# The samples' paged attention moved out of a stage of its own, into the mixer and the output projection of the prompt

## The chip, the core and the metric

The kernel runs on one core of one Trainium2 chip. The metric is the device time of one execution in microseconds (us). Before the change it is 3100.78 us, the median of three runs (3095.70 to 3108.07). Lower is better.

Engines: PE (TensorE, matrix products), ACT (ScalarE), DVE (VectorE), POOL (GpSimd), SP (SyncE, which here only issues transfers). Each works through its own list of instructions in the written order; they wait for one another by semaphores.

## The reference, cut to what matters

One inference step of a decoder with two layers, for a prompt group (1024 tokens) and a sample group (8 sequences of one new token). All is float32. In each layer:

```
h   = rmsnorm(x) * (1 + sc1) + sh1
aq, ak, av, af, bq, bk, bv, bg, ca, cb = split(h @ w_in)
o_a = attention of 4 heads x 128      (prompt: causal; samples: over 256 past rows + the new one)
o_b = retention, 4 heads x 64;  o_c = gated causal convolution, width 31
x   = x + g1 * rmsnorm(concat(o_a, o_b, o_c) @ w_o)
x   = x + g2 * rmsnorm(ffn(rmsnorm(x) ...))           (1024 -> 2 x 2816 -> 1024)
```

The change concerns the attention of the samples, which reads its past from pages (16 pages of 128 rows x 4 heads x 128, that is two for each of 8 samples), named by a page table:

```
k_all  = concat(cache_k[page_table], k_new);  v_all, lf_all likewise
cum    = cumsum(lf_all)
logits = (q . k_all) * scale + cum[new] - cum[key]
out    = softmax(logits) @ v_all              for 8 samples x 4 heads = 32 rows
```

## The kernel before

The program is a sequence of blocks; between two blocks all engines meet at a barrier. For each layer: `block_modulation`, `block_project`, `block_mixer`, `block_samples`, `block_tail`. Token columns are 1032: 1024 of the prompt and, at the end, 8 of the samples (`TP:NT`).

**Products in two parts.** Operands of the large products are split in a high and a low part (ACT writes `hi`, DVE or POOL subtracts for `lo`), and each product is three matmuls: hi x hi, lo x hi, hi x lo.

**`block_mixer`.** A loop over 42 *passes* (`p`), each a third of the columns for one of 14 weight tiles of `w_in`: 24 matmuls on `dense`. Between two passes PE does a step of the attention, which runs 9 passes behind: `phase(p)` gives the head `h` and the step `at`. So `p = 14` is head 0, step 5, `p = 23` head 1, step 5, `p = 37` head 3, step 1. Scores lie in the bank `sc`, DVE takes the top (`top_of`), ACT the exponential, DVE divides (`normalize`), PE transposes (`turn_probs`), ACT moves, PE multiplies with the values (`values`, into `o_bank`), DVE copies (`out_of`). SP loads the weight tiles in order (`load`, each waits until the tile two before it has been split) and stores K and V (`store`). `k.x` does not hold the residual here: it is parked in DRAM (`x_hold`), and its place holds q, k, v and the probabilities. `q_new`, `k_new`, `v_new` are the samples' columns, copied by `new_token`. In passes 1 to 12 DVE also does the last taps of the convolution (semaphore `tapped`).

**`block_samples`.** The samples' attention alone. SP loads 16 K pages and half of the V pages, ACT the 16 `lf` pages (log forget) and the other V pages. POOL spreads the query (`qd`), PE repeats it over all partitions (`q_bank`), DVE multiplies with K (`prod`) and sums (`lg`): 8 times. PE adds the bias (`b_bank`), turns the logits to 32 rows (`r_bank`), DVE and ACT do the softmax, PE turns it back (`t_bank`, `n_bank`) and multiplies: 16 matmuls with the weights in `pt` and 512 columns of V moving (`so_bank`), then four to turn the result (`q_bank`). Beside it SP loads and ACT and POOL split the first two tiles of `w_o` (`Ahead`), and SP loads the residual back into `k.x`.

**`block_tail`.** The output projection, then the feed-forward part, in two *halves* of the tokens: half 0 is 512 columns, half 1 is 520 with the samples. In half 0 and then half 1 PE goes through 8 *tiles* of `w_o` (`out_tile(hf, m)`, 24 matmuls in half 0, hooks `out_hook` before each `kk`). ACT runs `split(0)`, splits weight tile 2 (`high_to(2)`), then `split(1)`, then for each tile `finish(hf, m)`: square, copy, split the weight tile three ahead. DVE runs `lower(0)`, `lower(1)`, then `add_square`. Weight tiles pass through three buffers (`Stream`); SP loads them in order. `turn_context` (L1884) is a row of small matmuls between tiles 2 and 3. `joins[hf]` add the result to `k.x` later, in the time of the next half.

The places that the change and the steps below touch: `block_mixer` (L730; spread queries, K pages, two more weight tiles), `block_samples` (L1395, whole), `block_tail` (L1794; SP's list, `out_hook`, the ACT and DVE lists of half 0).

## Time and profile before

| what | us |
|---|---|
| median of three runs | 3100.78 |
| the profiled execution, whole | 3097.88 |
| its span, first to last instruction | 3096.1 |
| PE busy / DVE busy / ACT busy | 2880.4 / 1739.7 / 1171.4 |
| `block_samples` with its barriers, layer 0 (603.90 to 657.05) | 53.15 |
| the same, layer 1 (2130.00 to 2183.40) | 53.40 |
| half 0 of the output projection, layer 0 (657.05 to 712.00) | 54.95 |

The span is 1.78 us shorter than the execution. The mean granted TensorE clock is 0.948 of full speed. A matmul of float32 by float32 leaves two MATMUL records, one on split operands leaves one. A record's duration is a latency: matmuls overlap, so what a row of them costs is read from where the next row starts.

### The profile page before, as it was taken

Reading aid. Unit: us, or ns where it says so; the run is one execution under the profiler, and the core shown is the slowest. Engines: PE = TensorE matmul, PEld = TensorE weight load, DVE = VectorE, ACT = ScalarE, POOL = GpSimd, SP = SyncE. Lnnn points to the kernel's source line nnn. Section 1 sums busy time; section 2 is a strip of 40 time slices with the busy share of each in tenths; the row PEclk is TensorE's granted clock in tenths of the full one; section 3 lists DMA queues with packets and bytes.
Section 4 is the critical chain, followed back from the end, with each engine's and each line's share of the span. In section 5 each row is a group of like instructions: output and inputs, shape, how many; then the busy total and the mean of one; then the engine's idle time right before and its main releaser. Section 6 shows DMA issues by size and latency. Waiting matters only on the chain. (4 is left out here: it accounts for less than half of the span.)

```text
span 3096.1 us, 44175 instructions
## 1 busy us (share of the span) xinstructions
PE 2880.4 (93%) x17804; PEld 2467.3 (80%) x17804; DVE 1739.7 (56%) x2809; ACT 1171.4 (38%) x1863; POOL 335.9 (11%) x166
## 2 busy tenths in 40 slices
PE   6799999889999999999767999997999999999996
PEld 3587888658778889999726878885788788999995
DVE  1286433336676676676614944334266767676765
ACT  1222233424444445444312413333344444444442
POOL 4112010123000000000042210101320000000000
PEclk7799999989999999999868999997999999999998
DMA  8313111162323233323191221114422333332231
GB/s 313 132 41 107 36 35 35 50 200 79 95 89 95 89 96 96 89 89 96 38 341 51 92 49 36 35 28 144 137 75 89 96 96 92 92 96 89 89 96 65
DMA packets 366881, 293.29 MB, mean 95 GB/s; under 512 B 24189, under 2 KB 308389, under 8 KB 365886
## 3 DMA queue, kind: packets, MB, share of 16 engines
q1 hardware_dynamic: 355472, 284.18, 29.2%
q10 hardware_dynamic: 11214, 6.41, 0.7%
q8 instruction: 135, 2.21, 0.3%
q14 instruction: 60, 0.49, 0.1%
HBM read 267.68 MB, written 23.71 MB: 94 GB/s over the span
## 5 line engine op out<-in xcount | busy, mean ns | idle before, releaser
L1643 PE MATMUL tslot<-g_hi,w_hi 128*128 128x260 f32 (+1 forms) x2496 | 673.3, 324 | 7.6 <-DVE g_lo L2172 6.0
L1643 PE MATMUL tslot<-g_hi,w_lo 128*128 128x260 f32 (+1 forms) x2496 | 667.4, 322 | 0.0
L1643 PE MATMUL tslot<-g_lo,w_hi 128*128 128x260 f32 (+1 forms) x2496 | 665.4, 321 | 0.0
L1643 PEld LDWEIGHTS tslot<-g_hi,w_hi 128*128 128x128 f32 x2496 | 416.5, 190 | 48.7 <-DVE g_lo L2172 6.2
L1643 PEld LDWEIGHTS tslot<-g_hi,w_lo 128*128 128x128 f32 x2496 | 415.6, 190 | 38.0
L1643 PEld LDWEIGHTS tslot<-g_lo,w_hi 128*128 128x128 f32 x2496 | 415.8, 190 | 37.6
L1614 ACT ACTIVATE w_hi<-w_raw 128x1024 fp32r<-128x1024 f32 x292 | 307.1, 1052 | 317.5 <-PE tslot L1961 312.6
L2233 DVE TENSOR_TENSOR cat<-cat,tslot 128x512 f32<-128x512 f32 (+1 forms) x320 | 220.6, 690 | 192.1 <-PE tslot L1961 190.8
L1618 DVE TENSOR_TENSOR w_lo<-w_raw,w_hi 128x1024 fp32r<-128x1024 f32 x256 | 312.0, 1219 | 0.0
L1961 PE MATMUL tslot<-f_hi,w_hi 128*128 128x260 f32 (+1 forms) x1056 | 283.3, 323 | 6.0 <-DVE w_lo L1618 3.7
L1961 PE MATMUL tslot<-f_hi,w_lo 128*128 128x260 f32 (+1 forms) x1056 | 281.9, 322 | 0.0
L1961 PE MATMUL tslot<-f_lo,w_hi 128*128 128x260 f32 (+1 forms) x1056 | 280.9, 320 | 0.0
L2196 DVE SCALAR_TENSOR_TENSOR bufs<-bufs,vecs 128x512 f32<-128x512 f32 x176 | 132.1, 750 | 235.2 <-ACT bufs L2097 235.2
L854 PE MATMUL dense<-h_hi,w_hi 128*128 128x344 f32 x672 | 231.0, 344 | 5.3 <-PEq L2384 5.3
L854 PE MATMUL dense<-h_hi,w_lo 128*128 128x344 f32 x672 | 216.5, 322 | 0.0
L854 PE MATMUL dense<-h_lo,w_hi 128*128 128x344 f32 x672 | 216.4, 322 | 0.0
L1961 PEld LDWEIGHTS tslot<-f_hi,w_hi 128*128 128x128 f32 x1056 | 175.4, 190 | 26.9 <-DVE cat L2233 5.5
L1961 PEld LDWEIGHTS tslot<-f_lo,w_hi 128*128 128x128 f32 x1056 | 175.7, 189 | 16.0
L1961 PEld LDWEIGHTS tslot<-f_hi,w_lo 128*128 128x128 f32 x1056 | 176.2, 190 | 14.7
L505 DVE SCALAR_TENSOR_TENSOR cat<-cat,vecs 128x1023 f32<-128x1023 f32 (+14 forms) x120 | 176.3, 1469 | 3.3
L154 PE MATMUL slot<-h_hi,w_hi 128*128 128x260 f32 x528 | 119.6, 337 | 34.0 <-POOL h_lo L454 15.6
L2097 ACT ACTIVATE bufs<-bufs,vecs 128x520 f32<-128x520 f32 (+1 forms) x176 | 144.2, 820 | 18.2
(317 smaller groups left out, 4029.7 us busy)
## 6 DMA issues: line engine op xcount, KB each, us to landing
w_raw<-in_ffn_up_dram SPq DMA_DIRECT2D x176, 512.0 KB, 3.7
a_raw<-in_ada_w_dram SPq DMA_DIRECT2D x24, 2048.0 KB, 18.6
w_raw<-in_ffn_down_dram SPq DMA_DIRECT2D x88, 512.0 KB, 3.6
w_raw<-in_w_in_dram SPq DMA_DIRECT2D x46, 512.0 KB, 3.9
w_raw<-in_w_o_dram SPq DMA_DIRECT2D x32, 512.0 KB, 4.0
x_hold<-x_res SPq DMA_DIRECT2D x2, 4128.0 KB
x_res<-x_hold SPq DMA_DIRECT2D x2, 4128.0 KB, 16.0
kp<-in_cache_k_dram SPq DMA_DIRECT2D x32, 256.0 KB, 3.0
```

The costliest lines, as they stand in the source:

```text
L154: last = e.matmul(out[:, OFF + a:OFF + b], w[:, k, cols], x[:, k, a:b], start=(k == 0 and first), stop=(k == kt - 1 and w is w_lo))
L505: return dve.scalar_tensor_tensor(acc, u[:, 0:TP - CTX + w], k.vecs[:, 1, 2 * w + j:2 * w + j + 1], acc, ALU.mult, ALU.add)
L854: last = pe.matmul(dense[p % 2][:, 0:b - a], w[:, kk, :], x[:, kk, a:b], start=(kk == 0 and first), stop=(kk == KD - 1 and w is w_lo))
L1614: act.activation(self.hi[n % 3][:, :, :], self.raw[n % 3][:, :, :], ACT.Copy).then_inc(self.hi_done, 1)
L1618: e.tensor_tensor(self.lo[n % 3][:, :, :], self.raw[n % 3][:, :, :], self.hi[n % 3][:, :, :].bitcast(F32), ALU.subtract).then_inc(self.dve ...
L1643: last = pe.matmul(out[:, at + a:at + b], w[:, kk, :], x[:, kk, t0 + a:t0 + b], start=(kk == 0 and first), stop=(kk == KD - 1 and w is w_lo))
L1961: last = pe.matmul(out[:, at + a:at + b], w, x[e][:, a:b], start=first and name == pairs[0], stop=final and name == pairs[-1])
L2097: act.activation(t_ab[half][:, 0:w], raw[half][:, 2:2 + w], ACT.Identity, scale=vec[:, 3, c:c + 1], bias=vec[:, 3, c + 2 * FT:c + 2 * FT + ...
L2196: dve.scalar_tensor_tensor(tt[:, 0:512], r[:, 1:513], tap1, tt[:, 0:512], ALU.mult, ALU.add).then_inc(conv, 1)
L2233: dve.tensor_tensor(y_m, y_m, out[:, at:at + w], ALU.add).then_inc(gathered, 1)
```

## The change

`block_samples` is gone. Its work is spread over its two neighbours:

- **In the mixer.** The queries are repeated by PE from `q_new` itself (`spread_query`, four matmuls 128x128, one sample each), at eight passes, for one head and four samples at a time; DVE multiplies and sums there. K pages are loaded for one head at a time (16 transfers of 128 rows x 512 bytes), into a part of `k.cat` and, for head 3, of `k.x`, by SP between the weight tiles. The first two tiles of `w_o` pass through the mixer's own weight loop as tiles 14 and 15.
- **In half 0 of the output projection.** SP loads the 16 `lf` pages ahead of the weight tiles and the 16 V pages behind tile 4; PE's bias, rows, probabilities and values hang in `out_hook` at tiles 1, 2, 4 and in the middle of 5. The values are now 64 matmuls with V as the weights and one column moving. ACT and DVE take the small steps between tiles. The samples' columns of the first four groups of `k.cat` are split last (`split_samples`, `sample_low`), and half 1 waits for them (`samp_lo`).
- **The residual** returns in two transfers, by token half, in half 1, after the values are done, each with a semaphore (`x_back`).

```diff
@@ block_mixer
+        both_att = sb("att", [P, 2, 2, 2 * P])
+        att = [both_att[:, i, :, :] for i in range(2)]
+        prod = both_att[:, :, :, :].rearrange("p a b c -> p a (b c)")
+        pages = [k.cat[:, 4:6, 0:S * DA]] * 3 + [arena[:, 0:4 * NT].rearrange("p (a b) -> p a b", b=NT)[:, 0:4:2, 0:S * DA]]
+        SPREADS = {14: (0, 0), 20: (0, 1), 23: (1, 0), 29: (1, 1), 32: (2, 0), 33: (2, 1), 37: (3, 0), 38: (3, 1)}
...
+            def load_keys(h):
+                if h == 0:
+                    sp.wait_ge(tapped, 2 * CONV_W - TAPS_EARLY)
+                elif h < 3:
+                    sp.wait_ge(prod_done, 2 * h)
+                else:
+                    sp.wait_ge(scored, NC8 * 3)
+                    sp.wait_ge(turned, 9)
+                    sp.wait_ge(new_done, 9)
+                for n in range(S * NPG):
+                    sp.dma_start(pages[h][:, n % NPG, DA * (n // NPG):DA * (n // NPG) + DA],
+                                 d["cache_k"][L, bass.ds(page(n), 1), :, h, :].rearrange("o p n -> p (o n)")).then_inc(k_loaded[h % 2], 16)
...
-            for n in range(5, N_TILES):
+            for n in range(5, N_TILES + 2):
                 load(n)
+                if n in (6, 9, 12, 13):
+                    load_keys({6: 0, 9: 1, 12: 2, 13: 3}[n])
...
+            sp.wait_ge(lo_done, N_TILES + 1)
...
+                    if i == 0 and h in (1, 2):
+                        pe.wait_ge(prod_done, 2 * h)
...
+                    if i == 4 and h < 2:
+                        pe.wait_ge(prod_done, 2 * h + 1)
...
+            def spread_query(p):
+                h, half = SPREADS[p]
+                ph, at = phase(p)
+                pe.wait_ge(new_done, 3 * h + 2)
+                if h >= 2:
+                    pe.wait_ge(g_scaled, 12)
+                    pe.wait_ge(prod_done, 2 * h + half)
...
+                for j in range(4):
+                    s = 4 * half + j
+                    last = pe.matmul((x_bank if h >= 2 else o_bank)[:, P * j:P * j + P], k.q_new[:, h, s:s + 1].to_broadcast([P, P]), ident,
+                                     start=True, stop=True)
+                last.then_inc(q_spread, 1)
...
-                    if p % 3 == 2 and p // 3 + 2 < N_TILES:
+                    if p % 3 == 2:
                         high(p // 3 + 2)
...
+            def multiply(p):
...
+                dve.wait_ge(q_spread, 2 * h + half + 1)
+                dve.tensor_tensor(prod, pages[h][:, :, 512 * half:512 * half + 512], bc((x_bank if h >= 2 else o_bank)[:, :], 1, NPG),
+                                  ALU.mult).then_inc(prod_done, 1)
...
+            def reduce(p):
...
+                dve.tensor_reduce(k.lg[:, :, 4 * half:4 * half + 4, h], prod.rearrange("p g (s n) -> p g s n", n=DA), AX_X,
+                                  ALU.add).then_inc(lg_done, 1)
@@ block_samples: all removed
@@ block_tail, SP
             sp.dma_start(stage, d["state_ffn_conv"][L].rearrange("s r (c n) -> c (s r) n", n=P)).then_inc(s_ready, 16)
+            for n in range(S * NPG):
+                page = sp.value_load(k.pages[0:1, n:n + 1], min_val=0, max_val=N_POOL - 1)
+                sp.dma_start(lf[:, n // NPG, n % NPG, :], d["cache_logf"][L, bass.ds(page, 1)].rearrange(
+                    "o p h -> p (o h)")).then_inc(lf_loaded, 16)
...
+                    if (hf, m) == (0, 4):
+                        for n in range(S * NPG):
...
+                    if (hf, m) in ((1, 1), (1, 5)):
+                        back = int(m == 5)
+                        sp.wait_ge(v_summed, 1)
+                        sp.dma_start(k.x[:, :, joins[back].all], k.x_hold.rearrange("p (a b) -> p a b", b=NT)[:, :, joins[back].all]).then_inc(
+                            x_back[back], 16)
@@ block_tail, PE
+            def sample_bias():
+                ones, after = const(k, "ones"), const(k, "after")
+                pe.wait_ge(e_ready, 1)
+                pe.wait_ge(lf_loaded, 16 * S * NPG)
...
+            def sample_values():
+                pe.wait_ge(pt_moved, 1)
+                pe.wait_ge(v_loaded, 16 * S * NPG)
+                for h in range(HA):
+                    for s in range(S):
+                        for pg in range(NPG):
+                            last = pe.matmul(slot[2][:, BANK + S * h + s:BANK + S * h + s + 1], vp[:, s, pg, DA * h:DA * h + DA],
+                                             pt[:, pg, HA * s + h:HA * s + h + 1], start=(pg == 0), stop=(pg == NPG - 1))
+                last.then_inc(v_summed, 1)
...
+                    if (hf, m, kk) == (1, 0, 0):
+                        pe.wait_ge(samp_lo, 1)
+                    if hf == 0:
+                        step = {(1, 0): sample_bias, (2, 0): sample_rows, (4, 0): sample_probs, (5, 4): sample_values}.get((m, kk))
@@ block_tail, ACT
             for m in range(KD):
                 finish(0, m)
+                if m == 2:
+                    exp_samples()
...
+                if m == 6:
+                    split_samples()
@@ block_tail, DVE
             lower(0)
+            sample_bias()
             lower(1)
+            sample_logits()
             for m in range(1, KD):
                 add_square(0, m)
+                if m == 2:
+                    sample_top()
+                elif m == 3:
+                    sample_normalize()
+                elif m == 4:
+                    sample_turned()
+                elif m == 5:
+                    sample_out()
+                elif m == 7:
+                    sample_low()
+            dve.wait_ge(x_back[0], 16)
```

**SP at the start of the tail.** The list of SP before, layer 0: the context of the convolution, then the weight tiles of `w_o`.

```order
L131 DMA w_raw<-in_w_o_dram 128x8x128 x2
L1442 DMA x_res<-x_hold 128x8256
L1399 UNCONDITIONAL_BRANCH
L1847 UNCONDITIONAL_BRANCH
L1849 DMA rc<-in_state_ffn_conv_dram 44x16x128
L1604 DMA w_raw<-in_w_o_dram 128x8x128 x6
```

And after the change; the five rows from TENSOR_LOAD to DMA stand 16 times for `lf`, and 16 times in the same form for V:

```order
L1771 DMA rc<-in_state_ffn_conv_dram 44x16x128
L1773 TENSOR_LOAD pages
L1773 ISA x2
L1774 ISA
L1774 DMA bufs<-in_cache_logf_dram 128x4
...
L1512 DMA w_raw<-in_w_o_dram 128x8x128 x3
L1782 TENSOR_LOAD pages
...
L1783 DMA x_res<-in_cache_v_dram 128x512
L1512 DMA w_raw<-in_w_o_dram 128x8x128 x3
```

The first weight tile that the tail loads (tile 2) now stands behind 16 page loads.

**PE in half 0, the samples' last product.** Before it stood in a block of its own:

```order
L1473 MATMUL t_bank<-consts,rows 128x32 x2
L1474 MATMUL n_bank<-dnew,consts 128x32
L1481 MATMUL so_bank<-vpg,pt 32x512 x16
L1486 MATMUL q_bank<-consts,orow 128x8 x4
```

After the change it stands in the middle of tile 5:

```order
L1551 MATMUL tslot<-g_hi,w_hi 128x512
L1551 MATMUL tslot<-g_lo,w_hi 128x512
L1551 MATMUL tslot<-g_hi,w_lo 128x512
L1864 MATMUL tslot<-bufs,x_res 128x1 x64
L1551 MATMUL tslot<-g_hi,w_hi 128x512
```

Sixteen matmuls with 512 moving columns have become 64 with one, each with 128 columns of new weights.

**DVE in the mixer at pass 14 (head 0, step 5).** Before:

```order
L1290 TENSOR_SCALAR nb<-mx 128x1
L1308 SCALAR_TENSOR_TENSOR cat<-x_bank,cat 128x384
L1295 RECIPROCAL rr<-rs 128x1
L1297 TENSOR_SCALAR prob<-prob,rr 128x896
L1267 COPY q_new<-x_res 128x8
```

After:

```order
L1340 TENSOR_SCALAR nb<-mx 128x1
L1358 SCALAR_TENSOR_TENSOR cat<-x_bank,cat 128x384
L1407 TENSOR_TENSOR att<-cat,o_bank 128x1024
L1345 RECIPROCAL rr<-rs 128x1
L1347 TENSOR_SCALAR prob<-prob,rr 128x896
L1413 TENSOR_REDUCE lg<-att 128x2x4
L1317 COPY q_new<-x_res 128x8
```

The product stands ahead of the division by the row sum, the reduction behind it.

## Rows read from the trace of the kernel before

**Rows 1.** Windows by stage: length, PE busy (instructions), granted clock, DMA share, GB/s.
```profile
274.00:603.90 329.90, 325.48 (x2152) 0.99 0.14 38
603.90:657.05 53.15, 34.35 (x78) 0.74 0.75 258
657.05:712.00 54.95, 53.51 (x226) 0.91 0.38 106
...
2130.00:2183.40 53.40, 35.26 (x78) 0.71 0.74 257
```

**Rows 2.** Timeline, DVE, samples' stage: start, length, line, operation, idle before it.
```profile
603.57 0.29 DVE L1302 COPY cat<-o_bank 128x128 f32<-128x128 f32 x1 [4.58 <-PE o_bank L993]
605.18 0.19 DVE L1519 TENSOR_TENSOR e_new<-consts,logf 128x32 f32<-128x32 f32 x1 [1.32 <-PEq L2384]
...
612.92 1.21 DVE L1527 TENSOR_TENSOR prod<-kp,q_bank 128x1024 f32<-128x1024 f32 x1
614.17 1.22 DVE L1529 TENSOR_REDUCE lg<-prod 128x8 f32<-128x1024 f32 x1
```

**Rows 3.** Timeline of SP, the samples' stage and the start of the tail.
```profile
606.14 16.95 SPq L1436 DMA_DIRECT2D kp<-in_cache_k_dram  x16
...
657.05 0.37 SPq L1849 DMA_DIRECT2D rc<-in_state_ffn_conv_dram  x1
657.47 20.03 SPq L1604 DMA_DIRECT2D w_raw<-in_w_o_dram  x6
```

**Rows 4.** Window of 20 us in the mixer, PE alone.
```profile
560.00:580.00 20.00, 20.00 (x133) 1.00 0.18 54
```

**Rows 5.** Timeline of PE in the mixer, the attention steps around pass 35.
```profile
541.10 0.93 PE L979 MATMUL turn<-consts,prob 128*128 128x128 f32 x7
...
545.65 1.72 PE L993 MATMUL o_bank<-x_res,v_tok 128*128 128x128 f32 x14
547.21 1.04 PE L979 MATMUL turn<-consts,prob 128*128 128x128 f32 x8
```

**Rows 6.** Timeline of DVE in the mixer at passes 12 to 14.
```profile
372.86 1.25 DVE L505 SCALAR_TENSOR_TENSOR cat<-cat,vecs 128x994 f32<-128x994 f32 x1
...
393.73 0.56 DVE L1308 SCALAR_TENSOR_TENSOR cat<-x_bank,cat 128x384 f32<-128x384 f32 x1
394.91 0.16 DVE L1295 RECIPROCAL rr<-rs 128x1 f32<-128x1 f32 x1 [0.62 <-ACT prob L1138]
```

**Rows 7.** DMA issues: size of one, median us to landing.
```profile
kp<-in_cache_k_dram SPq DMA_DIRECT2D x32, 256.0 KB, 3.0
```

**Rows 8.** Timeline of ACT, start of the tail and finish of tile 3.
```profile
657.08 4.27 ACT L2037 ACTIVATE g_hi<-cat 128x512 fp32r<-128x512 f32 x8 [2.72 <-PEq L2384]
663.63 1.06 ACT L1614 ACTIVATE w_hi<-w_raw 128x1024 fp32r<-128x1024 f32 x1 [2.28 <-DMA w_raw<-in_w_o_dram]
...
689.69 0.60 ACT L2051 ACTIVATE bufs<-tslot 128x512 f32<-128x512 f32 x1 [10.56 <-PE tslot L1643]
```

**Rows 9.** Timeline of PE around `turn_context`, layer 0.
```profile
676.99 4.71 PE L1884 MATMUL tmisc<-consts,rc 44*128 44x44 f32 x32
681.63 0.79 PE L1643 MATMUL tslot<-g_hi,w_hi 128*128 128x512 f32 x1
```

**Rows 10.** Windows there; columns PE, PEld, DVE, ACT, POOL busy, then granted clock.
```profile
677.00:679.60 2.60, 2.60 (x25) 2.60 (x24) 0.69 (x1) 2.03 (x3) 0.50 (x2) 1.00 0.65 169
679.60:681.60 2.00, 2.00 (x11) 1.95 (x10) 0.00 (x0) 0.00 (x0) 1.95 (x1) 0.50 0.55 191
681.60:686.40 4.80, 4.80 (x12) 3.80 (x12) 0.00 (x0) 0.00 (x0) 0.00 (x0) 0.50 0.37 109
```

**Rows 11.** Windows of line L391, modulation; columns PE, PEld busy, granted clock.
```profile
101.90:102.75 0.85, 0.85 (x8) 0.85 (x8) 1.00 0.00 0
102.75:104.35 1.60, 1.60 (x10) 1.60 (x9) 0.50 0.00 0
```

**Rows 12.** Timeline of PE in the mixer, line L873.
```profile
281.62 2.03 PE L873 MATMUL o_bank<-cat,prob 64*64 64x1 f32 x64
```

More of the change, by code:

```diff
@@ L835, in _ @@
                 plink(pool.tensor_tensor(pre[:, HA * c:HA * c + HA], pre[:, HA * c - HA:HA * c], k.logf[:, HA * c - HA:HA * c], ALU.add))
-            for n in range(1, N_TILES):
+            for n in range(1, N_TILES + 2):
                 pool.wait_ge(hi_done, n)
@@ L1803, in block_tail @@
         diag = sb("diag", [P, 520])
-        v, y, t = (sb(n, [P, 5]) for n in ("jv", "jy", "jt"))
+        v, y, t = (k.ncum[:, 8 * n:8 * n + 5] for n in range(3))
         hs = diag[:, 0:KD * S].rearrange("p (k s) -> p k s", s=S)
@@ L1814, in block_tail @@
         ring, acc = [rc[:, i, :] for i in range(3)], rc[:, 3, :]
+        R = S * HA
+        vp = k.x[:, :, :].rearrange("p a b -> p (a b)")[:, 0:S * NPG * HA * DA].rearrange("p (s g n) -> p s g n", s=S, g=NPG)
+        lots = [raw[0][:, 2 + a:2 + b] for a, b in ((0, 257), (257, 289), (289, 321), (321, 385), (385, 417), (417, 449), (449, 453), (453, 517))]
+        rows, dnew, one = lots[0][0:R], lots[4][0:R], lots[6][0:R]
+        e_new, qk, vn = (lots[i].rearrange("p (s h) -> p s h", h=HA) for i in (1, 2, 5))
+        lf = lots[7].rearrange("p (s g h) -> p s g h", s=S, g=NPG)
+        pt = lots[3].rearrange("p (g r) -> p g r", g=NPG)
+        (v_loaded, lf_loaded, e_ready, b_ready, lg_ready, qk_ready, rows_ready, rows_link, neg_ready, exp_done, prob_ready, pt_ready, pt_moved,
+         v_summed, cat_done, samp_hi, samp_lo) = (k.sem(n) for n in (
+             "v_loaded", "lf_loaded", "e_ready", "b_ready", "lg_ready", "qk_ready", "rows_ready", "rows_link", "neg_ready", "exp_done",
+             "prob_ready", "pt_ready", "pt_moved", "v_summed", "cat_done", "samp_hi", "samp_lo"))
+        x_back = [k.sem(f"x_back{i}") for i in range(2)]
+        N_POOL = d["cache_v"].shape[1]
         st = Stream(k, k.w_raw, k.w_hi, k.w_lo)
@@ L2034, in split, with split_samples, exp_samples @@
             def split(hf):
-                cols = joins[hf].all
                 for kk in range(KD):
+                    cols = joins[hf].cols if kk < HA else joins[hf].all
                     act.activation(k.h_hi[:, kk, cols], k.cat[:, kk, cols], ACT.Copy).then_inc(x_hi, 1)
+            def split_samples():
+                act.wait_ge(cat_done, 1)
+                act.activation(k.h_hi[:, 0:HA, TP:NT], k.cat[:, 0:HA, TP:NT], ACT.Copy).then_inc(samp_hi, 1)
+            def exp_samples():
+                act.wait_ge(neg_ready, 1)
+                act.activation(rows, rows, ACT.Exp, bias=one[:, 1:2], accum_out=one[:, 2:3]).then_inc(exp_done, 1)
             def finish(hf, m):
@@ L2168, in lower @@
             def lower(hf):
-                cols = joins[hf].all
                 for kk in range(KD):
+                    cols = joins[hf].cols if kk < HA else joins[hf].all
                     dve.wait_ge(x_hi, KD * hf + kk + 1)
@@ new lines, in sample_logits, with sample_top @@
+            def sample_logits():
+                dve.wait_ge(b_ready, 1)
+                flat = k.lg[:, :, :, :].rearrange("p g s h -> p (g s h)")
+                dve.scalar_tensor_tensor(flat, flat, A_SCALE, slot[2][:, 0:NPG * R], ALU.mult, ALU.add).then_inc(lg_ready, 1)
+            def sample_top():
+                dve.wait_ge(rows_ready, 1)
+                link(dve.tensor_copy(rows[:, 0:PAST], slot[2][0:R, BANK:BANK + PAST]))
+                link(dve.tensor_scalar(rows[:, PAST:PAST + 1], slot[2][0:R, BANK + PAST:BANK + PAST + 1], A_SCALE, None, ALU.mult))
+                link(dve.tensor_reduce(one[:, 0:1], rows, AX_X, ALU.max))
+                dve.tensor_scalar(one[:, 1:2], one[:, 0:1], -1.0, None, ALU.mult).then_inc(neg_ready, 1)
@@ new lines, in sample_normalize, with sample_turned @@
+            def sample_normalize():
+                dve.wait_ge(exp_done, 1)
+                link(dve.reciprocal(one[:, 3:4], one[:, 2:3]))
+                dve.tensor_scalar(rows, rows, one[:, 3:4], None, ALU.mult).then_inc(prob_ready, 1)
+                dve.wait_ge(prob_ready, 1)
+                dve.tensor_scalar(dnew, const(k, "ident")[0:R, 0:R], rows[:, PAST:PAST + 1], None, ALU.mult).then_inc(prob_ready, 1)
+            def sample_turned():
+                dve.wait_ge(pt_ready, 1)
+                dve.tensor_copy(pt, slot[2][:, 0:NPG * R].rearrange("p (g r) -> p g r", g=NPG)).then_inc(pt_moved, 1)
+                link(dve.tensor_tensor(vn, k.v_new[:, :, :].rearrange("p h s -> p s h"),
+                                       slot[2][:, 2 * R:3 * R].rearrange("p (s h) -> p s h", h=HA), ALU.mult))
@@ new lines, in sample_out, with sample_low @@
+            def sample_out():
+                dve.wait_ge(v_summed, 1)
+                dve.tensor_tensor(k.cat[:, 0:HA, TP:NT], vn.rearrange("p s h -> p h s"),
+                                  slot[2][:, BANK:BANK + R].rearrange("p (h s) -> p h s", h=HA), ALU.add).then_inc(cat_done, 1)
+            def sample_low():
+                dve.wait_ge(samp_hi, 1)
+                dve.tensor_tensor(k.h_lo[:, 0:HA, TP:NT], k.cat[:, 0:HA, TP:NT], k.h_hi[:, 0:HA, TP:NT].bitcast(F32),
+                                  ALU.subtract).then_inc(samp_lo, 1)
```

212 lines of the change are left out of this document (58 added, 154 removed).

## The prediction

> **What bounds the kernel now.** I read the page first (busy shares, the slices), then windows by stage, then the timelines of the engines where the change cuts. PE is busy 93% of the span, so the question at each place is whether PE waits or works. The windows say where it does not work: in the mixer it is busy 325.5 of 329.9 us at a granted clock of 0.99, in the samples' stage 34.35 of 53.15 us (35.26 of 53.40 in layer 1) at 0.74 and 0.71, in half 0 of the output projection 53.51 of 54.95 [rows 1]. The two samples' stages, 106.55 us, are what there is to win. Both neighbours are bound by PE: 20 us in the mixer hold 20.00 us of PE [rows 4]. Whatever PE gets there lies on the path; whatever DVE, ACT or SP get may be hidden. The chain that ended last covers only the output of the result and says nothing here.
>
> The sum is made against the profiled execution, 3097.88 us (span 3096.1 and 1.78 around it); it lies 2.9 under the median of 3100.78.
>
> **Removed.** Stage and barriers, 53.15 and 53.40. One barrier stays: from the mixer's last copy, 603.57 + 0.29, to the first instruction of the next block, 605.18, that is 1.32 us [rows 2]. So 51.8 + 52.1 = 103.9 us go. With them goes the waiting for K, since K is now loaded passes ahead, and the transfer of the residual, which returns in the time of half 1 and isn't needed before the joins there: nothing is charged for it unless v_summed is late, and even then the first half (2 MB) has 15 us and more.
>
> **Mixer, added on PE.** Eight spreads per layer, each 4 matmuls of 128 columns with new weights, 8 records. Fourteen such records take 547.21 - 545.65 = 1.56 us, 0.111 each [rows 5]; a spread is 0.9 and with the change of operands 0.95 us. Eight are 7.6. PE has no idle time there, so all of it counts. The high parts of tiles 14 and 15 are two ACT instructions of 1.06 us [rows 8]; the second falls where the last head runs without passes to hide it, and I add 0.7. Mixer: 8.3 per layer, 16.6 in all. Bounds: nothing for the second term, 2 for late steps: 15 to 19, if DVE stays hidden.
>
> **Mixer, added on DVE and SP, taken as nothing.** A product is 1.21 and a reduction 1.22 us [rows 2], 16 pairs in all, 38.9 us. What hides them: at pass 14 DVE sits idle for 0.62 us ahead of the reciprocal while ACT does the exponential [rows 6], and what it makes there PE wants only after the next pass, some 3.8 us of matmuls (541.10 plus 7 x 0.11, to 545.65) [rows 5]. K of head 0 is issued when the last tap is done, 372.86 + 1.25 = 374.1 [rows 6]; sixteen page loads take 16.95 us [rows 3] and land 3.0 later [rows 7]: 394.1, against a product that starts near 394.8. Heads 1 and 2 have three passes as well, 20 us for 20. So there is no slack worth the name in the loads, but what is late by a microsecond delays DVE, not yet PE. If the cover is gone, each pair costs up to 2.43 us.
>
> **Half 0, step by step (layer 0, from SP's first transfer at 657.05).** What one tile takes: tile 3 runs from 681.63 [rows 9] to about 689.6, where ACT reads it [rows 8]; 4.8 us of it at half clock [rows 10], which cost 2.4. At full clock a tile is 5.6 us. Tiles 1 and 2 before 676.99 give the end of tile 0: 665.8, or 8.7 on this count.
>
> 1. *The wait for lf.* Sixteen page loads with their register loads took 16.95 us, (16.95 - 0.37)/15 = 1.10 each [rows 3]. Behind the first transfer they end near 17.7, and land near 20.5. PE stands at the head of tile 1 from 8.7 on: 11.8 us. Then it is cold: the bias' 10 records at 0.21 are 2.1, tile 1 loses 2.4. Together 16.3. The first weight tile for SP, tile 2, comes behind the same loads: issued 17.7, split by ACT from 23.9 (6.2 from issue to ACT, as 657.47 to 663.63 [rows 3, 8]), then 1.06, the split of half 1 like the 4.27 of half 0, and 1.1 for finish: 30.3. PE ends tile 1 at 30.6. So this second wait lies beside the first, and to take away one alone would gain little.
> 2. *Rows.* 6 records, 1.0.
> 3. *Probabilities.* DVE normalizes only after the square of tile 3: ACT 0.6, DVE some 0.7 for the addition (0.56 for 384 columns [rows 6]), then three small instructions. PE waits 2.5, then 6 records, 1.0: 3.5.
> 4. *Values.* 64 matmuls are 128 records, each with 128x128 of new weights and one column. The row nearest in form is L391: 8 records in 0.85 us at 2.4 GHz, 0.106 each; at 1.2 GHz 9 weight loads in 1.60, 0.18 each [rows 11]. In turn_context, 24 or 25 records take 2.6 us at full clock, and the last 8 the 2.0 us to 681.63, 0.25 each [rows 9, 10]. I take 0.11 and 0.21. Which clock? In turn_context PE and its weight loads were busy all the time (2.60 of 2.60), and the clock fell to 1.2 GHz after 2.6 us, and stayed there for 4.8 us of the next tile [rows 10]. So: about 3 us at full clock (27 records), 101 x 0.21 = 21.2, together 24.2; then 2.4 lost in the rest of tile 5. 26.6. Bounds: 128 x 0.11 = 14.1 with no loss after, and 128 x 0.25 + 2.4 = 34.
> 5. *The samples' low part.* Half 1 waits until tile 7 is squared, added, and the samples' columns subtracted: 1.9.
>
> Sum 16.3 + 1.0 + 3.5 + 26.6 + 1.9 = 49.3 per layer, 98.6 for two. The V loads (16 x 1.10 us on SP behind tile 4) end near 36, long before values at about 61, and weight tile 5 behind them is there near 40, wanted at 58.
>
> By the page "TensorE: Matmul & The Clock Gate" of the Trainium skill, section "What's actually happening", the clock follows how busy PE has been recently. Taken as busy share, that would keep it high in the values, and give the second case below; the row with PE and weight loads at 100% and a falling clock speaks against it. The same page, section "LDWEIGHTS (loading the stationary operand)", has a weight load cost its columns over 1.2, in ns, whatever the rows: 107 ns for 128. At full clock the trace agrees (0.106); at half it shows about twice that, so the rule's 13.7 us for the values is again the case of the clock that stays.
>
> **Total.** -103.9 + 16.6 + 98.6 = +11.3: 3109.2, rounded up for small waits to 3110. The whole stage removed is paid back, three quarters of the repayment (85.8 of 115.2 us) by two things: SP's page loads ahead of the weights, and matmuls that load 128 columns of weights to move one.
>
> **Rivals.**
> - *The clock stays high in the values.* Condition: weight loads count as work. For it: nothing in the trace shows so long a row of such records; against it, the fall in a short one [rows 10]. Values 14.1 in place of 24.2, no 2.4 after: -12.5 per layer, 3085.
> - *Small weight loads are cheaper.* 64 records with 64x64 weights took 2.03 us, 0.032 each [rows 12]; by that rate values are 4 us. These use a quarter of the array, and L391 has the right form, so it is unlikely. -22.6 per layer: 3065.
> - *The lf loads don't hold PE.* Condition: a page load alone on SP is much quicker than beside ACT's (both queues issued at once in the stage before). At half the pace the wait is some 8 us shorter; the whole of it with its cold start is 14.2. Between -16 and -28: 3088.
> - *DVE becomes the mixer's bound (the slow side).* Place: the division of the row sums behind the product, above all at passes 20, 29 and 38 where two are divided, and where K arrives late. It decides from the point where the division ends later than the pass that covers it: over about 3.8 us. Only the product stands ahead of the division: 16 x 1.21 = 19: 3129; with the reductions 3149. Against it: the idle time ahead of the reciprocal [rows 6] takes half a product.
>
> **How the numbers follow.** Forecast 0.62 (3110, own range 3098 to 3122); clock stays 0.12; cheap loads 0.03; lf quick 0.06; DVE bound 0.17. 0.5% of the median is 15.5 us, about what can be told from no change: faster is under 3085.3, slower over 3116.3. Faster: half of the second case and the lf case, the cheap loads, some mixtures: 0.18. Slower: a fifth of the forecast, and the DVE case: 0.29. Same: 0.53. Range 3080 to 3130: down to the clock case with part of the lf case, up to the product in the mixer's path.
>
> **What would show it.** After: no window between mixer and tail but a barrier of 1.3 us. In the tail, PE idle for about 12 us behind its first 24 matmuls, released by lf transfers; a row of 128 records with one column of about 24 us with a clock that falls after 3; half 0 near 104 us in place of 55. In the mixer, stages of about 338 us, PE still without idle time, spreads of 0.9. It is wrong if PE has idle time in the mixer released by DVE, if the values take 14 us, or if PE waits at tile 1 for much less than 12.

## The result and the profile after

| | us |
|---|---|
| before, 20 runs | 3096.22 (3092.26 to 3108.07) |
| after, 20 runs | 3111.20 (3102.34 to 3119.93) |
| ratio | 1.0044, interval 1.0034 to 1.0053 |
| forecast | 3110, range 3080 to 3130 |

The change costs 15.0 us by the medians. It is small, but the interval excludes equality. Against the 3100.78 of the first three runs, it is 10.4 us; the two profiled executions (3097.88 and 3108.57) differ by 10.7.

The stages after, as in [rows 1] (length, PE busy and its instructions, granted clock, DMA share, GB/s); the kernel after has no window between mixer and tail:

```profile
271.70:609.90 338.20, 333.26 (x2216) 0.99 0.19 53
611.15:718.36 107.21, 86.67 (x375) 0.75 0.39 117
1803.70:2141.40 337.70, 333.26 (x2216) 0.99 0.19 53
2142.69:2247.35 104.66, 83.94 (x375) 0.77 0.41 120
```

Between the last mixer instruction and the tail's first lie 1.28 us in either layer. So the balance, measured in the two profiles:

| term | forecast | measured |
|---|---|---|
| samples' stages gone | -103.9 | -104.0 (53.15 + 53.40 - 2 x 1.28) |
| mixer | +8.3 and +8.3 | +8.3 and +5.8 |
| half 0 | +49.3 and +49.3 | +52.5 and +53.0 |
| sum | +11.3 | +15.6 |

Half 0 is measured from SP's first transfer to PE's first matmul of half 1: 611.15 to 718.36 against 657.05 to 711.8, and 2142.69 to 2247.35 against 2183.34 to 2235.0 before. The rest of the program is 4.9 us shorter in the profile of after; no run explains that. It is less than such stretches scatter: from DVE's row `diag` (128x8) in half 1 of layer 0 to SP's first transfer in the tail of layer 1, where after, e2, e3, e7, e10 and e11 have the same code, their profiles have 1310.6 to 1321.4 us.

SP at the start of the tail (the list that answers to [rows 3]), start and length:

```profile
611.15 0.32 SPq L1771 DMA_DIRECT2D rc<-in_state_ffn_conv_dram  x1
612.51 16.91 SPq L1774 DMA_DIRECT2D bufs<-in_cache_logf_dram  x16
629.78 1.86 SPq L1512 DMA_DIRECT2D w_raw<-in_w_o_dram  x3
632.40 17.91 SPq L1783 DMA_DIRECT2D x_res<-in_cache_v_dram  x16
```

PE in half 0 and at the head of half 1, the rows where it waited, and the values:

```profile
630.86 0.60 PE L1837 MATMUL tslot<-bufs,consts 128*128 128x32 f32 x2 [11.13 <-DMA bufs<-in_cache_logf_dram]
644.32 1.03 PE L1847 MATMUL tslot<-consts,lg 128*32 128x128 f32 x4 [4.16 <-DVE lg L2183]
666.33 0.74 PE L1855 MATMUL tslot<-consts,bufs 32*128 32x32 f32 x4 [2.21 <-DVE bufs L2197]
678.64 22.68 PE L1864 MATMUL tslot<-bufs,x_res 128*128 128x1 f32 x128
718.36 0.48 PE L1551 MATMUL tslot<-g_hi,w_hi 128*128 128x260 f32 x2 [1.61 <-DVE g_lo L2212]
```

Four waits, 19.1 us in all (19.3 in layer 1), and a row of 128 records that takes 22.68 us (24.14 in layer 1). The rest of what half 0 got longer is small products, and matmuls at half clock behind each pause.

Windows of the values; columns PE, PEld, DVE, ACT, POOL busy, then granted clock:

```profile
678.60:681.60 3.00, 3.00 (x29) 2.96 (x28) 0.00 (x0) 0.00 (x0) 1.93 (x1) 1.00 0.00 0
681.60:701.20 19.60, 19.60 (x104) 19.60 (x103) 0.00 (x0) 0.00 (x0) 0.00 (x0) 0.55 0.00 1
```

PE never stops, and its clock falls nevertheless: a mean of 0.55 over 19.6 us is 1.0 for the first 2.0 of them and 0.5 (1.2 GHz) for the rest, so it fell some 5 us into the row.

In the mixer at pass 14, DVE (answers to [rows 6]):

```profile
393.25 1.22 DVE L1407 TENSOR_TENSOR att<-cat,o_bank 128x1024 f32<-128x1024 f32 x1 [0.40 <-PE o_bank L1080]
394.39 0.15 DVE L1345 RECIPROCAL rr<-rs 128x1 f32<-128x1 f32 x1
394.58 0.69 DVE L1347 TENSOR_SCALAR prob<-prob,rr 128x896 f32<-128x896 f32 x1
395.18 1.22 DVE L1413 TENSOR_REDUCE lg<-att 128x8 f32<-128x1024 f32 x1
```

The idle time of 0.62 us ahead of the reciprocal is gone: the product takes its place, and the reduction stands behind the division. The reciprocal starts 2.10 us behind the start of the operation of L1358 (392.29), where it was 1.18 before; PE shows no wait between 300 and 560 us all the same.

### The profile page after: what moved, and what is told of

It is laid out like the page before. It is cut to its first block and busy times, and to the rows that moved or that the text cites. A ratio compares the mean times of both kernels' runs of the same rounds, so it can differ in the third digit from the quotient of the medians.

```text
span 3106.8 us, 45241 instructions
## 1 busy us (share of the span) xinstructions
PE 2888.8 (93%) x18076; PEld 2518.0 (81%) x18076; DVE 1742.5 (56%) x2811; ACT 1169.9 (38%) x1863; POOL 317.0 (10%) x148
## 3 DMA queue, kind: packets, MB, share of 16 engines
q8 instruction: 137, 2.24, 0.3%
q10 hardware_dynamic: 4302, 2.15, 0.2%
```

## The experiments

Each edit is against the changed kernel ("after") unless said otherwise. Medians of the comparison's runs:

| kernel | median us | ratio to before | interval |
|---|---|---|---|
| after | 3111.20 | 1.0044 | 1.0034 to 1.0053 |
| lf pages early | 3073.11 | 0.9915 | 0.9902 to 0.9928 |
| weights first | 3116.72 | 1.0065 | 1.0050 to 1.0080 |
| values spread | 3099.38 | 1.0005 | 0.9992 to 1.0018 |
| lf early + values spread | 3067.83 | 0.9898 | 0.9884 to 0.9912 |
| DVE product twice | 3112.32 | 1.0050 | 1.0033 to 1.0068 |
| PE spreads twice | 3125.22 | 1.0092 | 1.0074 to 1.0110 |
| residual whole | 3108.16 | 1.0038 | 1.0025 to 1.0050 |
| residual later | 3104.85 | 1.0029 | 1.0014 to 1.0044 |
| values spread + residual later | 3084.20 | 0.9961 | 0.9946 to 0.9976 |
| lf early + values spread + residual later | 3050.93 | 0.9866 | 0.9842 to 0.9889 |
| the same, two steps later in their tiles | 3043.06 | 0.9830 | 0.9808 to 0.9852 |

**The lf pages early (e1).**

```diff
@@ block_mixer, SP, behind the last store
+            for n in range(S * NPG):
+                sp.dma_start(k.lf[:, n // NPG, n % NPG, :], ...cache_logf...).then_inc(lf_loaded, 16)
+            sp.wait_ge(lf_loaded, 16 * S * NPG)
@@ block_tail, SP
-            for n in range(S * NPG):
-                page = sp.value_load(k.pages[0:1, n:n + 1], min_val=0, max_val=N_POOL - 1)
-                sp.dma_start(lf[:, n // NPG, n % NPG, :], ...).then_inc(lf_loaded, 16)
@@ block_tail, PE, sample_bias
-                pe.wait_ge(lf_loaded, 16 * S * NPG)
```

> The 16 lf pages are loaded by SP at the end of the mixer, into a place of their own, and not at the head of the tail; PE's bias waits for none. My theory: PE's idle time behind its first 24 matmuls in half 0 (11.1 us in layer 0), the cold start after it, and the second wait inside the bias go, in both layers: about 16 us each, 3111 - 32 = 3079. Half 0 falls from 107 to about 91 us. Rival A, the pages only move the wait (the mixer's barrier now waits for them, or PE waits for the weight tile instead): under 5 us in all, 3106 to 3111. Rival B, the idle time costs nothing but itself: 2 x 11.1 = 22, 3089.

Measured: 3073.11, 38 under after and 6 under my theory. PE goes straight from tile 0 to the bias:

```profile
623.56 0.40 PE L1556 MATMUL tslot<-g_hi,w_lo 128*128 128x512 f32 x1
623.79 0.31 PE L1837 MATMUL tslot<-mod,consts 128*128 128x32 f32 x2
```

and half 0 takes 90.30 and 90.93 us, 16.9 and 13.7 shorter than after; the forecast's step 1 had 16.3. That is 30.6 of the 38; the other 7 were not found in a stage (the profiled execution of this kernel, 3080.7 in span, is as slow as the slowest of its five runs). Both rivals fall: the gain is larger than the bare idle time, and the wait does not move to the barrier or the weight tile.

**The weights first (e2).**

```diff
@@ block_tail, SP
-            for n in range(S * NPG):
-                page = sp.value_load(k.pages[0:1, n:n + 1], min_val=0, max_val=N_POOL - 1)
-                sp.dma_start(lf[:, n // NPG, n % NPG, :], d["cache_logf"][L, bass.ds(page, 1)]...).then_inc(lf_loaded, 16)
             for hf in range(2):
...
                     if (hf, m) == (0, 4):
+                        for n in range(S * NPG):
+                            page = sp.value_load(k.pages[0:1, n:n + 1], min_val=0, max_val=N_POOL - 1)
+                            sp.dma_start(lf[:, n // NPG, n % NPG, :], d["cache_logf"][L, bass.ds(page, 1)]...).then_inc(lf_loaded, 16)
```

> The weight tiles 2 to 4 are issued ahead of the lf pages, which now stand behind tile 4, right ahead of the V pages. The prediction said that the wait for weight tile 2 lies beside the wait for lf. My theory: PE still waits for lf at tile 1, and longer (tile 4's transfer waits for a buffer, so lf is issued only when tile 1 is split): as PE's bias stands ahead of tile 1, and the buffer of tile 4 is free once ACT and POOL have split tile 1, which they do at the start, the loads move some 3 to 6 us later: slower by 2 x 3 to 2 x 6, 3117 to 3123. Rival, the late weights are the cost of half 0 and not lf: faster by 10 or more, under 3101.

Measured: 3116.72, 5.5 slower than after, where the two intervals overlap by a hair, and far from the rival's 3101. The wait at the bias is 4.6 us longer, and the wait for the logits behind tile 1 (4.16 in layer 0 of after, 1.36 in layer 1) is gone:

```profile
636.59 0.60 PE L1837 MATMUL tslot<-bufs,consts 128*128 128x32 f32 x2 [15.74 <-DMA bufs<-in_cache_logf_dram]
```

So with lf late, early weights gain nothing in the balance. The edit moves both, and so prices neither alone: the wait for the logits, which my expectation left out, went, and kept the loss at its lower end (half 0 is 106.70 and 106.53 us).

**The values spread (e3).**

```diff
@@ block_tail, PE: 16 groups of 4 matmuls, ahead of kk = 4..7 of tile 5, 0..7 of 6, 0..3 of 7
-                step = {..., (5, 4): sample_values}.get((m, kk))
+                if 0 <= KD * (m - 5) + kk - 4 < 16:
+                    step = sample_values(KD * (m - 5) + kk - 4)
@@ block_tail, DVE
-                elif m == 5:
+                elif m == 6:
                     sample_out()
```

> The 64 matmuls of the values are cut into 16 groups of 4, each ahead of one kk step of tiles 5 to 7, so that 3 matmuls with 512 moving columns stand between two groups. My theory: the granted clock no longer falls, the 128 records take 0.11 us each, 14.1 us in place of 22.7 to 24.2, and tile 5 loses no 2.4 us at half clock: faster by 11 to 12.7 per layer, 3111 - 24 = 3087. The chain to the samples' low part is later by about one tile, which may cost up to 2 per layer. Rival, the price is the number of weight loads with one column whatever the clock: no gain, 3108 to 3114.

Measured: 3099.38, 11.8 under after: half of the forecast, and the interval lies apart from after's. The clock did what the theory said:

```profile
680.00:685.00 5.00, 5.00 (x36) 4.57 (x35) 0.00 (x0) 0.00 (x0) 0.76 (x1) 1.00 0.00 0
685.00:690.00 5.00, 5.00 (x35) 4.55 (x34) 0.69 (x1) 2.03 (x3) 2.38 (x1) 1.00 0.00 0
```

against 0.55 over the same stretch above. Tiles 5 to 7 with the values take 31.2 us (PE's idle time ahead of half 1 not counted); three times the 5.58 of tile 6 in after are 16.7, so the 128 records cost 14.5 us, 0.113 each, instead of 22.5 and a rest of tile 5 at half clock. Half 0 is 96.06 and 96.39 us, 11.1 and 8.3 shorter. But from half 1 of layer 0 to the tail of layer 1 the program is 8.3 us longer, and 4.4 behind half 0 of layer 1. The rows there, POOL and DVE, then PE:

```profile
715.05 2.39 POOL L1526 TENSOR_TENSOR w_lo<-w_raw,w_hi 128x1024 fp32r<-128x1024 f32 x1 [12.42 <-ACT w_hi L1522]
717.97 2.35 POOL L1526 TENSOR_TENSOR w_lo<-w_raw,w_hi 128x1024 fp32r<-128x1024 f32 x1 [0.52 <-ACT w_hi L1522]
```

```profile
714.92 0.17 DVE L164 SCALAR_TENSOR_TENSOR ncum<-ncum 128x4 f32<-128x4 f32 x1
715.12 2.34 DVE L165 SCALAR_TENSOR_TENSOR ncum<-ncum 128x4 f32<-128x4 f32 x1
...
718.09 2.77 DVE L1599 TENSOR_TENSOR diag<-consts,ncum 128x512 f32<-128x512 f32 x1
```

```profile
720.92 1.12 PE L1584 MATMUL tslot<-diag,consts 128*128 128x512 f32 x2 [2.26 <-DVE diag L1599]
```

An instruction on 128x4 elements takes 2.34 us, and ends when POOL's subtraction ends (715.05 + 2.39 = 717.44); the diagonal, 0.69 in after, ends half a microsecond behind the next. Why does POOL work just there? Because ACT split the weight tile late, and it waited for its transfer:

```profile
713.91 1.06 ACT L1522 ACTIVATE w_hi<-w_raw 128x1024 fp32r<-128x1024 f32 x1 [5.51 <-DMA w_raw<-in_w_o_dram]
```

SP had issued the residual's 2 MB at 703.71, ahead of that weight tile's load at 704.38; half 1 began at 708.9. In after the residual is issued at 701.35 and half 1 begins at 718.36, so there was room. The Trainium skill, page "SBUF — State Buffer", section "SBUF: two separate sides", says that DVE and GpSimd share one port pair as an exclusive lock: a DVE instruction with two SBUF inputs, behind a GpSimd one that reads SBUF, waits for its whole length. The trace agrees: the two ends lie 0.02 us apart.

What this meeting costs is read from a later row, which stands behind the norm of half 1; here in after, in this kernel, and in e11, which has the same short values and a later residual:

```profile
829.67 0.17 DVE L1597 TENSOR_TENSOR diag<-consts,ncum 128x8 f32<-128x8 f32 x1
824.33 0.17 DVE L1597 TENSOR_TENSOR diag<-consts,ncum 128x8 f32<-128x8 f32 x1
819.33 0.17 DVE L1597 TENSOR_TENSOR diag<-consts,ncum 128x8 f32<-128x8 f32 x1
```

From the first matmul of half 1 (718.36, 708.89, 707.99) that is 111.3, 115.4 and 111.3 us, and in layer 1 again 111.3, 115.4 and 111.3. So the residual's early place, by way of this meeting, costs 4.1 us in each layer, 8.2 in all. (In the other kernels but e4 this length is 111.3 or 112.9 to 113.0.) The other 4.2 of the 8.3 us lie farther behind, in code that the edit leaves as it was and that scatters by more (above).

**lf early and values spread (e4).**

> lf pages loaded at the end of the mixer, and the values in 16 groups of 4 between the kk steps. My theory: the two gains add, 3111 - 32 - 24 = 3055, faster than the kernel before (3096) by 40. Rival, one gain hides the other (half 0 is held by the samples' chain or the weight tiles, not by PE): not much better than the better of the two alone, 3079 to 3087.

Measured: 3067.83, only 5.3 under e1 and 13 over my theory. Half 0 is 75.63 and 81.14 us, so the two gains do add there (107.21 to 75.63 in layer 0). Again a part is lost behind it: from the head of half 1 to the tail of layer 1 it is 1436.5 us, against 1424.7 in e1. The residual's 4.1 are in that (115.4 us to the row shown above, 111.3 in e1); the rest lies in the stretch that scatters. The time lies between my theory and the rival's, 11 us from the rival's, and the rival's reason did not hold: half 0 was not held.

**DVE's product twice (e5).**

```diff
@@ block_mixer, DVE, multiply
+                dve.tensor_tensor(prod, ...the same operands..., ALU.mult).then_inc(prod_first, 1)
+                dve.wait_ge(prod_first, 2 * h + half + 1)
                 dve.tensor_tensor(prod, ..., ALU.mult).then_inc(prod_done, 1)
```

> Each of the 16 products with K on DVE in the mixer is done twice (the result is the same), 1.2 us more each, 19.4 us in all, ahead of the division of the row sums. My theory: DVE has cover, PE goes on without idle time, the time stays within 4 us of the changed kernel, 3108 to 3115. Rival, DVE is the mixer's bound at these passes: up to 19 us slower, 3120 to 3130; then PE shows idle time released by DVE between passes 14 and 38.

Measured: 3112.32, 1.1 over after: nothing that can be told apart. The added work is in the lines of its profile (busy us, mean ns, idle before):

```profile
L1411 DVE TENSOR_TENSOR att<-cat,o_bank 128x1024 f32<-128x1024 f32 x8 | 9.8, 1220 | 0.3
L1411 DVE TENSOR_TENSOR att<-x_res,x_bank 128x1024 f32<-128x1024 f32 x4 | 4.9, 1221 | 0.1
L1411 DVE TENSOR_TENSOR att<-cat,x_bank 128x1024 f32<-128x1024 f32 x4 | 4.9, 1220 | 0.1
```

19.6 us more on DVE, and none of it on the path. The prediction's slow rival has room to spare; it would take more than 1.2 us per product.

**PE's spreads twice (e6).**

```diff
@@ block_mixer, PE, spread_query
-                for j in range(4):
+                for j in (0, 1, 2, 3) * 2:
```

> Each spread of the queries is done twice on PE (8 matmuls for 4, the result is the same). My theory: PE is the path in the mixer, so 8 x 0.95 us per layer more, 15 us in all: 3126. Rival, the spreads lie in time that PE would wait anyway: no change, 3111. The two mixer stages should be longer by 7.6 us each.

Measured: 3125.22, 14.0 over after. In the lines by operation, the kernel after and then this one:

```profile
L1080 PE MATMUL o_bank<-consts,q_new 128*128 128x128 f32 x64 | 8.8, 281 | 0.0
L1080 PE MATMUL x_bank<-consts,q_new 128*128 128x128 f32 x64 | 8.6, 278 | 0.0
```

```profile
L1080 PE MATMUL o_bank<-consts,q_new 128*128 128x128 f32 x128 | 16.0, 278 | 0.0
L1080 PE MATMUL x_bank<-consts,q_new 128*128 128x128 f32 x128 | 15.8, 277 | 0.0
```

14.4 us more busy time, 14.0 more in the median. From PE's first matmul of the mixer to SP's first transfer of the tail it is 349.2 and 346.3 us, against 339.4 and 338.9 in after; without any edit this length scatters too (342.6 and 339.1 in the two layers of e10). Every microsecond given to PE in the mixer counts, none given to DVE up to 20 does.

**The residual whole (e7), and later (e10).**

```diff
@@ e7, block_tail, SP: one transfer of the whole at (1, 1); DVE's second wait goes
-                    if (hf, m) in ((1, 1), (1, 5)):
+                    if (hf, m) == (1, 1):
@@ e10, block_tail, SP
-                    if (hf, m) in ((1, 1), (1, 5)):
+                    if (hf, m) in ((1, 2), (1, 5)):
```

> The residual comes back in one transfer of 4.1 MB at tile 1 of half 1 with one signal, not in two halves. In the changed kernel the first half is issued 17 us before half 1 begins, and takes about 10 to land; the whole would take some 20, and the weight tile behind it is wanted about 8 us into half 1, 25 us after the issue. My theory: hidden, 3108 to 3114. Rival, it is late here as the first half was with the spread values: ACT's split and POOL's subtraction shift onto DVE's norm chain, 3 to 12 us slower per layer, 3117 or more.

> The changed kernel with one edit: the first half of the residual is fetched behind weight tile 2 of half 1. My theory: it was hidden at its old place as long as the values took 23 us, so the time stays, 3107 to 3114. Rival, the transfer held the weights there already: 5 us or more faster.

Measured: 3108.16 and 3104.85. The whole is not slower than two halves; it takes 12.4 us from issue to landing (median), not the 20 I had expected, and the weight tile behind it is in time. So the splitting into two halves with a signal each buys nothing that can be seen in this kernel. e10 lies 6.3 under after, outside the range of my theory and inside the rival's. But its interval overlaps that of after, and its profile shows no gain where the transfer stands: from half 1 to the row of e3, 111.3 and 112.9 us, against 111.3 and 111.3 in after. So neither is shown.

**Values spread and the residual later (e11).**

> The changed kernel with the values spread in 16 groups of 4 and the residual's first half fetched behind weight tile 2 of half 1, lf pages as they were. With the values spread alone, half 0 was 11.1 and 8.3 us shorter by the profiles, yet 8.3 and 4.4 us were lost behind it. My theory: the whole gain arrives, 3111 - 20 = 3091 (3086 to 3093). Rival, most of it is lost elsewhere whatever the place of the residual: 3096 to 3100.

Measured: 3084.20, 27.0 under after, more than my 20. Half 0 is 92.96 and 91.53 us, 14.2 and 13.1 shorter than after, together 27.4. That the two numbers agree is in part chance: the profiled execution is only 15.6 us shorter than that of after, as other stretches of it are longer, and it lies 8.8 over its kernel's median. In e3 the same half gained 19.4 by the profile. Of the difference, 4.6 us are the wait for the logits at tile 2: 4.10 and 3.85 us there, 1.72 and 1.62 here. It is drawn by lot, as the next section shows. The residual's place itself is worth the 8.2 us behind half 0 that the rows in e3 show; the 15.2 between the medians of e3 and e11 hold the lot and the scatter besides. On its own (e10) the profile shows nothing for it. It is a cost only once the values are short.

**All three (e8), and two steps later in their tiles (e9).**

```diff
@@ e8 = e4 with the residual as in e10
@@ e9 = e8, and block_tail, PE
-  {(1, 0): sample_bias, (2, 0): sample_rows, (4, 0): sample_probs}
+  {(1, 0): sample_bias, (2, 4): sample_rows, (4, 4): sample_probs}
```

> As the kernel with early lf pages and spread values, and the first half of the residual is fetched behind the weight tile 2 of half 1, not ahead of it. Its traces showed why spreading the values gave only half of what half 0 got shorter: the residual's 2 MB stand ahead of a weight tile that is now wanted sooner; ACT splits it 2.5 to 3 us later, POOL's subtraction falls on DVE's chain for the norm (an instruction of 0.16 us took 2.34, the diagonal 2.77 for 0.69), and PE waits 2.26 us for it. My theory: 3 to 6 us per layer come back, 3068 - 9 = 3059. Rival, the loss in half 1 has another cause (DVE and POOL meet there anyway): 3064 to 3070.

> As the one before, and PE's rows and probabilities of the samples stand at kk = 4 of tiles 2 and 4, not at their head, 2.8 us later each. My theory: the waits there (2.2 us for the probabilities in both layers, up to 2.1 for the rows in one) go, and the half stays warm: 5 to 8 us better than the kernel before it, 3052. Rival, the samples' chain is the bound and the wait only moves (to the values at tile 5 or to the low part ahead of half 1): no gain, 3059.

Measured: 3050.93 and 3043.06. e8 is 16.9 under e4, twice my estimate. The diagonal is back at its length,

```profile
692.39 0.69 DVE L1604 TENSOR_TENSOR diag<-consts,ncum 128x512 f32<-128x512 f32 x1
```

and from the first matmul of half 1 to the row of e3 it is 111.3 and 112.9 us, against 115.4 and 117.0 in e4. These 8.1 us are what I had expected; the rest of the 16.9 was not found in a stage (the two kernels' five runs reach from 3049.40 to 3062.12 and from 3062.48 to 3070.80). e9 gains 7.9 more by the medians, with five runs each that overlap (3039.24 to 3051.86). By the profile half 0 is 10.5 us shorter in the two layers, since the rows and probabilities no longer find PE ahead of DVE:

```profile
607.36:680.47 73.11, 70.39 (x375) 0.93 0.49 146
2111.68:2183.77 72.09, 69.06 (x374) 0.95 0.49 148
```

That is half 0 with all of the samples' work in it, 73.11 us against 107.21. Between its first matmul and the last ahead of half 1, PE's timeline shows no wait at all; 1.60 us stand at half 1's head. This kernel is faster than both, by 54 us than before (3097.04 in the same comparison), ratio 0.983.

## Why the prediction was right

**The frame.** It was made as a sum of a stage that goes (103.9, measured 104.0), PE time that comes into the mixer, and PE time and waits that come into half 0. All three had the right sign and size; 11.3 against 15.6 in the profiles and 15.0 in the medians. Inside half 0 the steps were less good than their sum.

**The mixer.** Spreads of 0.95 us, eight per layer: shown by e6, which doubled them and cost 14.0 for 15.2. DVE hidden: shown by e5. The sum, 8.3 per layer, measured 8.3 and 5.8, which differ by less than a mixer scatters (e6); the term of 0.7 for a late split of the last tile can't be told from how PE's clock stands in the last head (DVE's last copy there waited 3.75 us for PE in layer 0 and 4.58 in layer 1).

**Half 0, by its steps**, layer 0:

| step | forecast | measured |
|---|---|---|
| 1: wait, cold bias, cold tile 1 | 11.8 + 2.1 + 2.4 | 11.1 + 2.1 + 1.6 |
| 2: rows | 1.0 | 4.2 wait + 1.0 + 2.1 cold |
| 3: probabilities | 3.5 | 3.3 + 2.9 cold |
| 4: values, cold rest of tile 5 | 24.2 + 2.4 | 22.5 + 1.4 |
| 5: low part | 1.9 | 1.6 |
| sum | 49.3 | 53.8 |

The cold parts are what a tile took over 5.57 us, at half clock (1.2 GHz). Against the sum, `turn_context` and tile 3 took 11.1 us here (653.03 to 664.12) and 12.5 before (676.99 to 689.49), which leaves the 52.5 by which the stage grew, to 0.1.

Step 1 was shown by e1 (30.6 us in two layers for 32.6 forecast). Step 4 by e3 and e11: with the clock up, the 128 records take 14.5 us, and by the medians of e11 the program is 27 us faster, the residual's place included, where the rival "the clock stays high" had worked out 25. That rival was thus right in its price and wrong in its condition: in the row of 128 the granted clock fell with PE and its weight loads busy all of the time. Part of that was luck. The forecast took the fall from one short row, `turn_context` in layer 0 [rows 10]. The same 32 records in layer 1 of the kernel before held 2.4 GHz, and so did the tile behind them; the prediction does not mention that:

```profile
2203.29:2206.99 3.70, 3.70 (x34) 3.65 (x33) 0.69 (x1) 2.03 (x3) 2.03 (x2) 1.00 0.93 283
```

Both rows of 128 in after did lose it: the mean granted clock over them is 0.61 and 0.57. Not tried was the old form of the values in the new place, 16 matmuls with 512 moving columns. In the stage before they took 16.06 us at a mean granted clock of 0.86, so it is open whether they would beat the 14.5:

```profile
637.68 16.06 PE L1481 MATMUL so_bank<-vpg,pt 128*32 128x512 f32 x32 [2.25 <-DMA vpg<-in_cache_v_dram]
```

The other three rivals fell by the trace: a record of 128x128 weights costs 0.21 us at 1.2 GHz and not 0.03, the lf pages came no faster on SP alone (16.91 us for 16, where the 16 K pages took 16.95 in [rows 3]), and DVE is not the bound.

**The steps that were short** are step 2, by 6.3 us, and step 3, where I counted the wait but not tile 4 at half clock behind it, 2.9. These 9.2 us were offset by luck: the other terms were 4.7 too long in all (1.5 in step 1, 2.7 in step 4), and the 1.4 of `turn_context` and tile 3 were not foreseen. That is why 49.3 came so near to 52.5.

In step 2 I counted the records and no wait. ACT's chain behind the late weight tile was as the prediction had it (ACT's copy of tile 0 ends at 639.67, PE's tile 1 at 640.16). But ahead of the logits DVE subtracts the eight low parts of half 1 (`lower(1)`), here in the two layers of after:

```profile
635.06 8.87 DVE L2163 TENSOR_TENSOR g_lo<-cat,g_hi 128x512 fp32r<-128x512 f32 x8 [18.10 <-ACT g_hi L2016]
...
2166.59 6.71 DVE L2163 TENSOR_TENSOR g_lo<-cat,g_hi 128x512 fp32r<-128x512 f32 x8 [18.09 <-ACT g_hi L2016]
```

and POOL the weight tiles 2 and 3:

```profile
634.59 2.40 POOL L1526 TENSOR_TENSOR w_lo<-w_raw,w_hi 128x1024 fp32r<-128x1024 f32 x1 [39.59 <-ACT w_hi L1522]
640.69 5.45 POOL L1526 TENSOR_TENSOR w_lo<-w_raw,w_hi 128x1024 fp32r<-128x1024 f32 x2 [3.71 <-ACT w_hi L1522]
```

Undisturbed, DVE's eight take 4.90 us (for half 0, at 611.83). POOL's first subtraction, begun 0.47 us ahead of them, holds them up by 1.8. POOL's next begins 5.63 us behind DVE's first, with the last of DVE's still to come. DVE's eighth, begun some 0.4 us behind it, takes 2.84 us in layer 0 and 0.69 in layer 1, 2.15 apart (8.87 against 6.71 for the eight); in layer 1 POOL's two take 6.13 us instead of 5.45. So one or the other waits, as if by who gets in first; but POOL begins 0.40 us ahead of DVE's eighth in one layer and 0.39 in the other, and the trace does not show what decides. In the two layers of all twelve kernels with the dissolved stage the eight take either 6.70 to 6.72 us (13 times) or 8.86 to 8.92 (11 times), and nothing between. In after, e3, e5, e6, e7, e10 and e11, which load both lf and weights late, PE waits 1.36 to 2.33 us for the logits with the first and 3.85 to 4.61 with the second. I had all of that at nothing. The late weights place it where PE waits for it: in e2 they are early, DVE and POOL meet all the same (6.71 and 6.70 us), but while PE still waits for lf. It is the same meeting of POOL and DVE as in e3.

In layer 1 of after the short wait gained nothing, since the next one was longer, 5.17 us for the probabilities instead of 2.21:

```profile
2194.75 1.03 PE L1855 MATMUL tslot<-consts,bufs 32*128 32x32 f32 x4 [5.17 <-DVE bufs L2197]
2187.96 1.06 ACT L1522 ACTIVATE w_hi<-w_raw 128x1024 fp32r<-128x1024 f32 x1 [6.73 <-DMA w_raw<-in_w_o_dram]
2191.72 2.47 POOL L1526 TENSOR_TENSOR w_lo<-w_raw,w_hi 128x1024 fp32r<-128x1024 f32 x1 [0.28 <-ACT w_hi L1522]
2192.10 2.24 DVE L2195 TENSOR_SCALAR bufs<-bufs 32x257 f32<-32x257 f32 x1
```

ACT waited for a weight tile ahead of the exponential, and DVE's division took 2.24 us beside POOL, 0.34 in layer 0. The other profiles with this wait have 2.2 to 2.3 us there. Over after, e5, e6, e7 and e10, half 0 takes 107.2 to 109.0 us where the eight took 8.9, and 102.6 to 106.4 where they took 6.7.

**What the prediction called it**: "The whole stage removed is paid back, three quarters of the repayment (85.8 of 115.2 us) by two things". Removing these two things, and the residual's transfer that comes into their place, turned +15 into -46 (e8), with the same dissolved stage. The change as such is worth having; its two costs sit in the order of SP's list and in a row of matmuls that stands in one piece.

## What to carry to other kernels

Work moved off its own stage costs what it takes on the engine that is the bound there, so price it by that engine alone and try the others by doubling them: here 19.6 us on DVE cost nothing and 14.4 on PE cost 14.0. Here 128 records with one moving column cost 22.5 us in a row and 14.5 dealt out between wide ones. When a stage gets shorter, look again at each transfer whose place was harmless only because the stage was long.

## What was not expected of the hardware

- PE's clock fell with PE and its weight loads busy all of the time, in a row of 128 one-column matmul records (granted clock 0.55 over 19.6 us); dealt out in groups of 8 records with 3 matmuls of 512 columns between, the granted clock stayed at 1.00 (e3, 680 to 690 us). In a row of 32 records with 44x128 weights and 44 moving columns it fell in one layer of the kernel before (0.78 over the row) and not in the other (1.00).
- A DVE instruction on 128x4 elements took 2.34 us instead of 0.16 while POOL subtracted 128x1024 elements, and DVE ended within 0.02 us of POOL.
- A transfer of 4.1 MB took 12.4 us from issue to landing, where its halves took 8.5 and 9.9.
- The same eight DVE instructions beside the same POOL instructions took 6.7 or 8.9 us, between layers of one execution and between executions, though POOL's second began 5.63 us behind them in both layers of after; PE's wait for the logits moved with it from 1.36 to 4.16 us.
- Sixteen small page loads (128x4 elements) take SP nearly as long as sixteen of 256 KB, 16.91 and 17.91 us: it is the issue that takes 1.06 to 1.12 us each, hardly the bytes.
